# Gate/up products of block 1 as pairs of 64-row matmuls over both banks of a panel

## The reference, cut to what matters

```python
def swiglu(h, w_gu, w_down):
    gu = h @ w_gu
    g, u = jnp.split(gu, 2, axis=-1)
    return (jax.nn.silu(g) * u) @ w_down

# in each layer l of block 1
x = x + 0.5 * mod[:, 2][:, None, :] * swiglu(h, w_ffn1_gu[l], w_ffn1_down[l])
...
x = x + 0.5 * mod[:, 8][:, None, :] * swiglu(h, w_ffn2_gu[l], w_ffn2_down[l])
```

## Time and profile before

| | us |
|---|---|
| median of 3 runs | 3669.26 (3668.59 to 3672.66) |
| span of the profiled execution | 3665.2 |
| TensorE busy | 3609.4 |
| VectorE busy | 1825.1 |
| GpSimd busy | 1621.2 |
| ScalarE busy | 1426.8 |

### The profile page before, as it was taken

How to read it: one execution, slowest core, us unless ns; L and a number is a source line. 1 busy time by engine, 2 the same in 40 slices (tenths; PEclk the granted TensorE clock), 3 DMA queues, 4 the chain that set the end, 5 groups by cost and what they waited for, 6 DMA issues and landing times.

```text
span 3665.2 us, 65989 instructions
## 1 busy us (share of the span) xinstructions
PE 3609.4 (98%) x25844; PEld 3005.3 (82%) x25844; DVE 1825.1 (50%) x3439; ACT 1426.8 (39%) x2027; POOL 1621.2 (44%) x1330
## 2 busy tenths in 40 slices
PE   7999999999999999999999999999999999999998
PEld 6888878888888887888897767888889988888887
DVE  6435565554775655763645444444427433343333
ACT  4322364322432245432234444443436533435333
POOL 2444444445454444445541003345458843334543
PEclk9999999999999999999999999999999999999999
DMA  8665525575555442445420001122245522212332
GB/s 258 190 186 162 149 59 161 184 223 168 183 176 189 151 115 65 157 155 159 139 74 20 15 25 36 58 94 90 90 136 165 159 69 70 75 58 92 92 99 85
DMA packets 560423, 442.81 MB, mean 121 GB/s; under 512 B 60452, under 2 KB 558157, under 8 KB 559949
## 3 DMA queue, kind: packets, MB, share of 16 engines
q1 hardware_dynamic: 560205, 439.73, 39.0%
HBM read 432.65 MB, written 2.83 MB: 119 GB/s over the span
## 4 chain that ended last, share of the span: by engine, by line
PE 92%; DVE 3%; ACT 2%; issue 1%; POOL 1%; SPq 1%; DMA 0%; DVEq 0%; ACTq 0%; POOLq 0%
PE ps_all L2603 26%; PE ps_all L2604 25%; PE ps_all L2605 25%; PE ps_all L2106 2%; PE ps_all L2124 1%; PE ps_all L2588 1%; PE ps_all L2085 1%; PE ps_all L2575 1%; PE ps_all L2089 1%; PE ps_all L2236 1%; PE ps_all L2576 1%; PE ps_all L2256 1%; POOL w_lo L1012 1%; DVE prod_t L3549 0%; PE ps_all L2219 0%
## 5 line engine op out<-in xcount | busy, mean ns | idle before, releaser
L1012 POOL TENSOR_TENSOR w_lo<-raw,w_hi 128x512 fp32r<-128x512 f32 (+2 forms) x1124 | 1341.5, 1225 | 1882.2 <-ACT w_hi L1589 1802.2
L2603 PE MATMUL ps_all<-h_hi,w_hi 128*128 128x512 f32 (+1 forms) x2600 | 1010.4, 389 | 2.8 <-POOL w_lo L1012 2.2
L2605 PE MATMUL ps_all<-h_hi,w_lo 128*128 128x512 f32 (+1 forms) x2600 | 1004.1, 386 | 0.0
L2604 PE MATMUL ps_all<-h_lo,w_hi 128*128 128x512 f32 (+1 forms) x2600 | 1003.9, 386 | 0.0
L1589 ACT ACTIVATE w_hi<-raw 128x2048 fp32r<-128x2048 f32 (+4 forms) x277 | 471.4, 1702 | 1275.5 <-PE ps_all L2605 1268.4
L2603 PEld LDWEIGHTS ps_all<-h_hi,w_hi 128*128 128x128 f32 x2600 | 488.7, 188 | 111.0 <-issue 11.1
L2605 PEld LDWEIGHTS ps_all<-h_hi,w_lo 128*128 128x128 f32 x2600 | 488.6, 188 | 98.7
L2604 PEld LDWEIGHTS ps_all<-h_lo,w_hi 128*128 128x128 f32 x2600 | 488.9, 188 | 96.9
L2603 PE MATMUL ps_all<-hid_hi,w_hi 128*128 128x512 f32 (+1 forms) x1282 | 473.2, 369 | 2.1 <-POOL w_lo L1001 1.7
L2605 PE MATMUL ps_all<-hid_hi,w_lo 128*128 128x512 f32 (+1 forms) x1282 | 469.5, 366 | 0.0
L2604 PE MATMUL ps_all<-hid_lo,w_hi 128*128 128x512 f32 (+1 forms) x1282 | 469.4, 366 | 0.0
(11 more groups left out here) (460 smaller groups left out, 5129.0 us busy)
## 6 DMA issues: line engine op xcount, KB each, us to landing
raw<-in_w_ffn_gu_dram SPq DMA_DIRECT2D x88, 1024.0 KB, 5.2
g_raw<-in_w_mod_dram SPq DMA_DIRECT2D x66, 1024.0 KB, 7.4
raw<-in_ffn_w_in_dram SPq DMA_DIRECT2D x54, 1024.0 KB, 5.0
g_raw<-in_ada_w_dram SPq DMA_DIRECT2D x48, 1024.0 KB, 5.3
raw<-in_w_ffn_down_dram SPq DMA_DIRECT2D x32, 768.0 KB, 4.7
raw<-in_w_ffn_down_dram SPq DMA_DIRECT2D x32, 640.0 KB, 4.3
raw<-in_ffn_w_out_dram SPq DMA_DIRECT2D x22, 768.0 KB, 4.7
raw<-in_ffn_w_out_dram SPq DMA_DIRECT2D x20, 640.0 KB, 4.3
```

The lines of the kernel that those rows point to most:

```text
L1012: ins = nc.gpsimd.tensor_tensor(v(w_lo), raw_view(st, i, j)[:, first:end, :], v(w_hi).bitcast(F32), ALU.subtract)
L2603: nc.tensor.matmul(o, whi, mhi, start=first, stop=False)
L2604: nc.tensor.matmul(o, whi, mlo, start=False, stop=False)
L2605: return nc.tensor.matmul(o, wlo, mhi, start=False, stop=last)
```

## The change

In gate/up steps without a convolution, every iteration but the first behind a norm runs the new function `by_row_halves`. A matmul over 128 rows is replaced by two over 64 rows, which are issued one behind the other: rows 0 to 63 write bank c = 0 and rows 64 to 127 write bank c = 1 (t is the row half). That gives each bank one half of its sum. A second pass with the banks swapped adds the other half. The order is: gate first halves, up first halves, gate swapped halves, up swapped halves. The waits for w_split_lo, g_read and product stand before the first halves, panel_used is counted at the end of the swapped halves, and the swapped halves wait for the end of the first ones of the same panel by a new counter, halves_made.

```diff
+                def by_row_halves(i):
+
+                    views = [[w_view(t, j, st["shapes"][j]) for t in (w_hi, w_lo)] for j in range(2)]
+                    rows_ = [slice(t * HD, (t + 1) * HD) for t in range(2)]
+                    if st is streams[2]:
+
+                        pe.wait_ge(sem["hc_in"], KD // 2)
+                    for swapped in range(2):
+                        for j, bank in enumerate((ps_g, ps_u)):
+                            if not swapped:
+                                read = ("g_read", "product")[j]
+                                pe.wait_ge(sem["w_split_lo"], p0 + i * 2 + j + 1)
+                                pe.wait_ge(sem[read], b[read] + i)
+                            else:
+                                pe.wait_ge(sem["halves_made"], b["halves_made"] + 2 * (i - st["wait_h"]) + j + 1)
+                            whi, wlo = views[j]
+                            for k in range(KD):
+                                mhi, mlo = (t[:, k * N:(k + 1) * N] for t in (h_hi, h_lo))
+                                for n, (wt, m) in enumerate(((whi, mhi), (whi, mlo), (wlo, mhi))):
+                                    for t in range(2):
+                                        c = 1 - t if swapped else t
+                                        ins = nc.tensor.matmul(bank[:, c, 0:N], wt[rows_[t], k, c * P:(c + 1) * P], m[rows_[t], :],
+                                                               start=(swapped == 0 and k == 0 and n == 0), stop=(swapped == 1 and k == KD - 1 and n == 2))
+                            ins.then_inc(sem["panel_used" if swapped else "halves_made"], 1)
+
                 def one(i, last):
+                    if st["conv"] is None and not (st["pre"] and isinstance(i, int) and i == 0):
+                        by_row_halves(i)
+                        return
                     for j, bank in enumerate((ps_g, ps_u)):
```

More of the change, by code:

```diff
@@ L148, in gu_step @@
                 dma=lambda i, j: [(None, wp[:, :, ds((j if conv is None else 1 - j) * FF + k0 * P + (i * 2 if j else i) * (P if j else 2 * P), 2 * P)])],
-                totals=dict(g_read=n // 2, product=n // 2, hid_hi=n // 2, hid_lo=n // 2,
+                totals=dict(g_read=n // 2, product=n // 2, hid_hi=n // 2, hid_lo=n // 2, halves_made=0 if conv is not None else 2 * (n // 2 - norm_first),
                             g_affine=n // 2 if conv is not None else 0, g_conv=n // 2 if conv is not None else 0,
```

## The result

| | before | after |
|---|---|---|
| median, us | 3668.9 (3667.5 to 3672.7, 4 runs) | 3784.7 (3782.4 to 3787.4, 4 runs) |
| span of the profiled execution, us | 3665.2 | 3785.5 |
| granted TensorE clock, mean | 0.994 | 0.992 |

The ratio is 1.0318, with a 95% interval of 1.0304 to 1.0333: 116 us more. The forecast was 3786. The profiled execution after took 3787.37 us, 1.9 more than its span.

What follows compares the result with a forecast made beforehand. TensorE's own rate was taken as the bound, with the splits hidden. Late slots (116 us) plus pairs (0) on 3669.3 us gave 3785, stated as 3786; range 3745 to 3850.

Steps and rivals of the forecast that it cites:

- Part 1: Gate and up slots come free later and are needed a quarter later, so splits delay TensorE: 116 us more.
- G before E: ScalarE starts on a used gate panel (G) 5.45 us before it starts on a used up panel (E).
- E to E, steady: From one ScalarE start on a used up panel to the next: 24.79 us against 21.76.
- 36 steady iterations: Changed gate/up iterations that cost the full 3.03 us each, 109 us together.
- first iteration of a second half: No gate wait and a split of 7.04 us: 1.5 us more, four times, 6 us.
- Part 2: 3840 matmuls become 3840 pairs of 64-row matmuls, a pair taking 0.227 us: near nothing, 0 in the sum.
- the low end: Rival: a pair loses the fp32r surplus and takes 0.2145 us, about 3749 us in all; chance 0.13.
- the high end: Rival: each half pays the surplus in turn, a pair takes 0.240 us, about 3822 us in all; chance 0.12.
- the up wait: TensorE's wait for the split of the next up panel in a steady iteration: 1.0 us.
- Halves one behind the other: Rival: fp32r halves do not run together, a pair takes 0.454 us, about 4540 us in all; chance 0.05.
- Not slower: Rival: pairs at or below 0.184 us, or splits fitting into a quarter (3622 us); chance 0.02.
- The clock: Rival: TensorE's clock falls at each iteration's waits, 26 to 61 us more, 3812 to 3847; chance 0.08.

Runs made afterwards that it cites:

- hid_lo_late: Changed kernel, but the DVE makes hid_lo only after the gemv work that follows, ahead of the next iteration's product: 3747.5 us.
- early_release_all: Changed kernel with every slot handed back in halves and split in two parts, also where old code or a down step used it last: 3669.0 us.
- full_rows_new_order: Changed kernel with full 128-row matmuls instead of the pairs, its order and semaphores kept: 3784.8 us.
- early_release: Changed kernel with slots handed back in halves and split in two parts, except where old code or a down step used the slot last: 3692.4 us.
- six_and_six: Changed kernel, but six matmuls of rows 0 to 63 are issued, then six of rows 64 to 127: 3829.6 us.
- half_after_half: Changed kernel, but all 24 matmuls of rows 0 to 63 of a panel's pass are issued, then the 24 of rows 64 to 127: 4305.8 us.

## Why the prediction was right

**What bounds.** Confirmed: w_hi and w_lo last as before, and all that is added, but for some 5 us of clock falls, is TensorE waiting for w_lo or restarting behind it.

**Part 1, term by term.**

| term | predicted | measured |
|---|---|---|
| G before E | 5.45 | 5.44 to 5.50 |
| E to E, steady | 24.79 | 24.72 to 24.82 |
| 36 steady iterations | +109 | 36 x 2.99 = +108 |
| first iteration of a second half | 23.80, 4 x 1.5 = +6 | 23.74 to 23.77, where it was 21.70 to 22.34: +6.5 |
| down step's first panel | +1 | at most +0.1 each, below +1 |
| clock falls in block 1 | none added | 4 more: 1.4, 1.6, 1.6 and 0.7 us, +5 |
| sum | 116 | 120 for the 120.3 between the two profiled spans; 116 between the medians |

The terms came out because they were built from one iteration's durations and not from busy shares: 5.04 and 6.04 us of split and 1.92 of w_hi against a quarter of 5.45. hid_lo_late shows that the uneven pair of waits was put down to the right causes, and early_release_all shows that nothing else of size is in the 116. That the forecast of 3786 meets the median to 1 us is partly luck: in the one pair of executions that is profiled the same terms make 120, and the 5 us of clock falls in it were not in the sum.

**Part 2.** Taken was 0.227 for a pair, by argument and with no row of fp32r row halves behind it; the trace after has 0.227 and full_rows_new_order gives the same total without pairs. Both bounds were off: the low end (0.2145) asked that the surplus over 512 columns goes with fewer rows, the high end (0.240) that it is paid twice. Neither happens, on fp32r operands.

**What was off.** The total of TensorE's waits for w_lo was forecast as 90 to 120 us and is 88, because the profile's idle time begins at a modelled end and leaves out 0.16 us of each wait. The up wait is 0.78 + 0.1 by start times where I had 1.0. The four first changed iterations have one wait of 2.5 to 2.6 us and not two of 2.0 and 1.0; their sum came out because the up split alone sets it. The lower end of the clock's price, 0.7 x 36, is 25 us and not 26.

**The rivals.** Pair at the low or the high end: out, by full_rows_new_order. Halves one behind the other (4540): out, the second of a pair starts at most 57 ns behind the first, in three quarters of the pairs 3 or 4. Not slower: out; the splits did not fit into a quarter; of what was tried only handing the slots back earlier was not slower. The clock: as a price of every iteration it is out, since in the trace after it fell in 4 of 40. But what was left out of the sum is not nothing: three of the four falls stand at the long waits of 2.5 to 2.6 us behind the old code, and early_release has a fall at all four of its own. In six_and_six, with the gate waits as they were, no up waits, and the first slots behind a wait half empty, it fell in 24 of 40; that the half empty slots did it is only argued. By themselves they don't: half_after_half, whose slots are half empty nearly throughout and which has hardly a wait, had no fall between its first and last product.

## What to carry to other kernels

Two interleaved uses of single-slot operands cost the engine that uses them nothing by themselves; here the whole cost came from the refill, which no longer fitted. For each slot write down when it comes free, when it is wanted again, and how long the refill takes, and do it for the first and last iteration too, where the slot's predecessor is another piece of code. If the refill is longer than that gap, hand the slot back in parts. Row-half pairs in the place of full-height matmuls change nothing here (3784.7 against 3784.8 us). Where a matmul has only 64 rows anyway, show two halves running together; no run here tries it on fp32r.

## What the runs showed of the hardware that I had not expected

- A row half's matmuls do not wait for all earlier matmuls of the other half. Issued in blocks of three they still run fully together (3789 us), and in blocks of 24 about 3.3 of them overlap at each change; blocks of six (3830 us) lose some 7 slots an iteration, which I can't explain. The Trainium skill (TensorE: Matmul & The Clock Gate, Part 3, packing small matmuls) says that matmuls start and end strictly in the order of the program; by that rule blocks of 24 would share at most the one slot at a change, 4 x (48 - 2) x 0.227 = 41.8 us from E to E. The trace has 37.52, so for row halves the starts are not in that order.
- The two of a pair start 3 or 4 ns apart in three quarters of the 3840 pairs, up to 57 ns in the rest, and the next pair comes 227 ns later, exactly as full matmuls do. The same part of the Trainium skill says that a weight load overlaps with a running matmul only when its row group differs, by which the 12 ns that an fp32r matmul takes beyond half an fp32 pass of 512 columns (227 against 214.5 ns) might have gone. They did not.
- hid_lo and the split slow each other: 0.96 us on GpSimd's side, 0.17 on the DVE's (1.35 against 1.18 us).
